# Interleaving the FFN weight tiles in pairs, so that TensorE loads its weights with a step of two elements

## The reference

```python
def swiglu(u, wg, wu, wd):
    return (jax.nn.silu(u @ wg) * (u @ wu)) @ wd      # u: 256 x 1024, wg, wu: 1024 x 2816, wd: 2816 x 1024
```

## Time and profile before

| what | value |
|---|---|
| median of three runs | 2071.14 us |
| the profiled execution, its own time | 2068.39 us |
| its span, first to last instruction | 2066.6 us |
| mean granted TensorE clock | 0.98 of full |
| TensorE matmuls / weight loads | 15720 / 15720 |
| VectorE busy | 1438.2 us (70%) |
| ScalarE busy | 1020.5 us (49%) |
| moved by DMA | 466.35 MB, mean 226 GB/s |

### The profile page before, as it was taken

One profiled execution on the slowest core, in us unless ns is written; L12 is line 12 of the kernel. 1 busy time (PEld: TensorE's weight loads), 2 busy tenths in 40 slices (PEclk: granted clock), 3 DMA queues, 4 the chain that ended last, 5 costly groups with the idle time before them and its releaser, 6 DMA issues.

```text
span 2066.6 us, 37422 instructions
## 1 busy us (share of the span) xinstructions
PE 1958.1 (95%) x15720; PEld 1905.4 (92%) x15720; DVE 1438.2 (70%) x2203; ACT 1020.5 (49%) x1568; POOL 116.3 (6%) x113
## 2 busy tenths in 40 slices
PE   3999899989999999999999979999999899999999
PEld 3999899989999999899899979998999898989998
DVE  5777687776676676968776757665677776756554
ACT  4454556454544444664545455453545454525553
POOL 0000002200000000022000010000000100000000
PEclk8999999999999999999999999999999999999999
DMA  8777565567776776755577746465578654554552
GB/s 348 271 270 281 196 237 197 185 215 255 255 285 211 251 274 224 260 188 215 185 284 268 282 171 217 158 219 209 202 265 284 231 205 164 206 192 176 200 190 99
DMA packets 83848, 466.35 MB, mean 226 GB/s; under 512 B 9440, under 2 KB 9568, under 8 KB 44512
## 3 DMA queue, kind: packets, MB, share of 16 engines
q1 hardware_dynamic: 46496, 326.00, 44.1%
q10 hardware_dynamic: 37184, 137.97, 18.6%
HBM read 462.88 MB, written 1.05 MB: 224 GB/s over the span
## 4 chain that ended last, share of the span: by engine, by line
PE 84%; DVE 8%; ACT 4%; DMA 2%; issue 1%; POOL 1%; ACTq 0%; DVEq 0%; SPq 0%
PE bank L646 83%; DVE low L1560 3%; DVE ada_ring L1542 1%; DMA region<-ada 1%; ACT high L1126 1%; DVE u_split L1603 1%; PE bank L915 1%; DVE tmp L1598 1%; DMA ring<-stream 0%; ACT u_split L1164 0%; POOL region L2046 0%; DVE region L1974 0%; DVE region L1929 0%; ACT rs L1147 0%; DVE region L1690 0%
## 5 line engine op out<-in xcount | busy, mean ns | idle before, releaser
L646 PE MATMUL bank<-u_split,high 128*128 128x256 f32 x6464 | 1147.9, 283 | 50.2 <-DVE u_split L1603 43.7
L646 PEld LDWEIGHTS bank<-u_split,high 128*128 128x128 f32 x6464 | 994.3, 190 | 61.1 <-DVE u_split L1603 36.6
L1560 DVE TENSOR_TENSOR low<-ring,high 128x1024 fp32r<-128x1024 f32 (+1 forms) x600 | 732.4, 1229 | 374.0 <-issue 224.0
L646 PE MATMUL bank<-u_split,low 128*128 128x256 f32 x3232 | 906.4, 280 | 0.0
L1126 ACT ACTIVATE high<-ring 128x1024 fp32r<-128x1024 f32 (+1 forms) x600 | 602.5, 1046 | 103.3 <-PE bank L646 87.7
L646 PEld LDWEIGHTS bank<-u_split,low 128*128 128x128 f32 x3232 | 615.3, 190 | 0.4
L646 PE MATMUL bank<-hid,high 128*128 128x256 f32 x2112 | 368.3, 279 | 0.0
L646 PEld LDWEIGHTS bank<-hid,high 128*128 128x128 f32 x2112 | 320.9, 188 | 0.0
L1542 DVE SCALAR_TENSOR_TENSOR ada_ring<-ada_ring,cond 128x1024 f32<-128x1024 f32 x242 | 298.1, 1233 | 0.0
L646 PE MATMUL bank<-hid,low 128*128 128x256 f32 x1056 | 295.0, 279 | 0.0
L646 PEld LDWEIGHTS bank<-hid,low 128*128 128x128 f32 x1056 | 200.4, 190 | 0.0
(11 more groups left out here) (186 smaller groups left out, 1642.3 us busy)
## 6 DMA issues: line engine op xcount, KB each, us to landing
ring<-stream SPq DMA_DIRECT2D x302, 1024.0 KB, 5.8
ada_ring<-ada ACTq DMA_DIRECT2D x242, 512.0 KB, 4.4
region<-ada ACTq DMA_DIRECT2D x7, 1024.0 KB, 22.3
ring<-stream SPq DMA_DIRECT2D x4, 640.0 KB, 4.2
region<-na_bias ACTq DMA_DIRECT2D x2, 1024.0 KB, 5.9
ring<-stream SPq DMA_DIRECT2D x4, 512.0 KB, 3.9
cst<-const ACTq DMA_DIRECT2D x1, 1600.0 KB, 21.1
cond<-cond SPq DMA_DIRECT2D x2, 512.0 KB, 7.5
```

The source lines that it names most:

```text
L646: return pe.e.matmul(out, lhs, rhs, start=start, stop=stop, skip_group_check=True)
L1560: dve.e.tensor_tensor(lo, src, hi.bitcast(F32), ALU.subtract).then_inc(*dve.done(("low", n)))
```

## The change

The two tiles 2j and 2j+1 of an FFN fill, which lay one behind the other, now lie woven: column 0 of the first, column 0 of the second, column 1 of the first, and so on. The host does this in `block`. The fills of FFN weights are marked `woven=True`; the fills of the mixers stay as they were. A tile is now read with the new view `Memory.woven(n, k)`: 128 elements at a step of two, starting at the pair's first or second element. The number, order, size and waits of all instructions on all engines and queues stay the same, and so do the sizes and the addresses of all transfers and buffers.

```diff
 class Fill:
-    def __init__(self, *parts):
-        self.parts = parts
+    def __init__(self, *parts, woven=False):
+        self.parts, self.woven = parts, woven
...
-        return np.concatenate(whole, axis=1).reshape(-1)
+        whole = np.concatenate(whole, axis=1)
+        if self.woven:
+            whole = whole.reshape(P, -1, 2, P).transpose(0, 1, 3, 2)
+        return whole.reshape(-1)
...
     def ffn(self, f, gate, up, down, layer, up_col):
         for n in range(FT):
-            both = self.fill_of((gate, layer, 0, KT, P * n, P), (up, layer, 0, KT, up_col + P * n, P))
+            both = self.fill_of((gate, layer, 0, KT, P * n, P), (up, layer, 0, KT, up_col + P * n, P), woven=True)
...
-            fill = self.fill_of(*tiles_[n:n + 2 * TILES])
+            fill = self.fill_of(*tiles_[n:n + 2 * TILES], woven=True)
...
+    def woven(self, n, k):
+
+        s = n % GRAINS * GRAIN + k // 2 * 2 * P
+        return [x[:, s:s + 2 * P].rearrange("p (n two) -> p two n", two=2)[:, k % 2, :] for x in (self.high, self.low)]
...
-                        t = mm3(b[:, i * T:(i + 1) * T], [x[:, k, :] for x in gs[i][1]], (m.uh[:, k, :], m.ul[:, k, :]),
+                        t = mm3(b[:, i * T:(i + 1) * T], m.woven(gs[i], k), (m.uh[:, k, :], m.ul[:, k, :]),
...
-                    t = mm3(b[:, i * T:(i + 1) * T], [x[:, k, :] for x in g], (m.uh[:, k, :], m.ul[:, k, :]),
+                    t = mm3(b[:, i * T:(i + 1) * T], m.woven(r, k), (m.uh[:, k, :], m.ul[:, k, :]),
...
-            t = mm3(b[:, 0:T], [x[:, at % TILES, :] for x in g], [x[:, k, :] for x in m.hid], k == 0, k == FT - 1)
+            t = mm3(b[:, 0:T], m.woven(r, at % TILES), [x[:, k, :] for x in m.hid], k == 0, k == FT - 1)
```

More of the change, by code:

```diff
@@ L126, in fill, with fill_of @@
         return self.fill_of(what)
-    def fill_of(self, *parts):
-        self.fills.append(Fill(*parts))
+    def fill_of(self, *parts, woven=False):
+        self.fills.append(Fill(*parts, woven=woven))
         return len(self.fills) - 1
@@ L741, in ffn @@
             if n == 0:
-                gs = [grain("gate", f, n), grain("up", f, n)]
+                gs = [grain("gate", f, n)[0], grain("up", f, n)[0]]
                 for k in range(KT):
@@ L745, in ffn @@
                     for i in range(2):
-                        t = mm3(b[:, i * T:(i + 1) * T], [x[:, k, :] for x in gs[i][1]], (m.uh[:, k, :], m.ul[:, k, :]),
+                        t = mm3(b[:, i * T:(i + 1) * T], m.woven(gs[i], k), (m.uh[:, k, :], m.ul[:, k, :]),
                                 k == 0 and i == 0, k == KT - 1)
-                t.then_inc(*pe.done(("read", gs[0][0]), ("read", gs[1][0]), ("full", "hid", f, n)))
+                t.then_inc(*pe.done(("read", gs[0]), ("read", gs[1]), ("full", "hid", f, n)))
                 continue
             for i, what in enumerate(("gate", "up")):
-                r, g = grain(what, f, n)
+                r, _ = grain(what, f, n)
                 for k in range(KT):
-                    t = mm3(b[:, i * T:(i + 1) * T], [x[:, k, :] for x in g], (m.uh[:, k, :], m.ul[:, k, :]),
+                    t = mm3(b[:, i * T:(i + 1) * T], m.woven(r, k), (m.uh[:, k, :], m.ul[:, k, :]),
                             k == 0, k == KT - 1)
@@ L758, in ffn @@
             if at % TILES == 0:
-                r, g = grain("down", f, at // TILES)
+                r, _ = grain("down", f, at // TILES)
             if k == 0:
```

## The result

The changed kernel takes 2112.52 us, the median of four runs (2111.83 to 2113.44 us). The kernel before took 2073.09 us in four runs beside it (2065.86 to 2075.61 us). The ratio is 1.0199, with a 95% interval from 1.0157 to 1.0241: slower by about 2%, clear of the noise. The time lies in the forecast range of 2050 to 2115 us, near its upper end, but that range was wide enough to take in a rival; the forecast itself, no change, was wrong.

The account below looks back on a forecast made before the run. The prediction took TensorE's pace in the six FFNs, load and matmul nearly balanced, as the bound. Four terms of 0 us left the profiled 2068.39 us, plus 2.75 us to the median: 2071 us, own range 2060 to 2082, with rivals 2050 to 2115.

Parts of the forecast that it names:

- parts (1) to (3): Host layout and transfers; the split on ScalarE and VectorE; queues, waits and matmuls: each forecast at 0 us.
- The two paces: FFN matmul pitches before the change: 5376 matmuls at the fast pace, 4128 at the slow one, 4.4 ns apart.
- The sum of 1093.6 us: Six unbroken TensorE runs in the chain, one per FFN, added up; more than half of the span.
- part (4): The 9504 FFN weight loads at a step of two: bounded from -18 to 1007 us, taken as 0.
- slack of 1 ns: In the FFNs at the fast pace, load alone 112.2 ns against matmul alone 113.3 ns per pitch.
- The second argument: FFN loads take elements at half the moving operand's rate, so a slower address step has room to hide.
- Rival A: FFN loads cost a few nanoseconds more and the slow pace holds everywhere: +24 us, 2095 us; chance 0.20.
- Rival B: FFN loads pay for skipped elements or no longer start beside the matmul before: +1007 us, about 3080 us; chance 0.10.
- Rival C: The FFNs' slow pace, if two reads meeting in memory, ends with another address order: -18 us, 2053 us; chance 0.24.

Follow-up runs that it names:

- down_woven: Changed kernel with only the down parts woven, gate and up dense as before: 2083.28 us, ratio 1.0087 to the kernel before.
- tiny_woven: Changed kernel with 24 extra matmuls of 32 columns ahead of each of two gate groups per FFN: 2166 us.
- some_woven: Changed kernel with the gate part of two hidden tiles per FFN split into matmuls of 128 columns: 2150 us.
- step3: Changed kernel with dense layout, each FFN load reading every third element, so products are of other weights: 2626 us.
- step4: Changed kernel with four tiles woven instead of two, so a load reads every fourth element: 3198 us.
- some_dense: Kernel before with the gate part of two hidden tiles per FFN split into matmuls of 128 columns: 2095 us.
- halves_dense: Kernel before with every FFN matmul of 256 columns split into two of 128, each with its own load: 5019 us.
- halves_woven: Changed kernel with every FFN matmul of 256 columns split into two of 128, each with its own woven load: 5022 us.

## Why the prediction was wrong

**What held.** TensorE's pace in the six FFNs is the whole matter. Layout, transfers, split, waits and queues cost nothing, as parts (1) to (3) had it: VectorE's busy time moved by 0.1 us, and in down_woven the dense parts kept their paces. Load and matmul run side by side and nearly at balance, 112 against 113.3 ns, so that "a nanosecond more per load costs up to 9504 x 0.001 = 9.5 us" was the right exchange rate. The two paces and their shares, 5376 and 4128, are those of the trace, and carried the account to 45.1 us of 45.0. The last 0.1 is partly luck, since the FFNs themselves grew by 44.3. The sum of 1093.6 us for the six FFNs misses the first 48 matmuls of two of them; it is 1107.7, and nothing in the forecast hangs on it.

**The step that failed** is part (4), "the value I take is 0, by the nearest row". The row was that the moving operand takes 1024 bytes in one pitch of 113.3 ns, and that a woven load spans the same. I named the load "another read path" and then gave it the moving operand's speed. The runs show the load's own: 64 pieces in 117.8 ns, in some stretches 120.0 (tiny_woven, some_woven), against 111.7 dense, and 1.8 to 1.9 ns for each further piece (step3, step4). The error is 4 to 7 ns above a pitch of 113, small as a rate and large against a slack of 1 ns (1.6 by the stretches of some_dense), which stood in the same paragraph. The second argument, that the load takes elements at 0.83 ns where the moving operand manages 0.44, counted elements, and what is paid for is pieces.

**Rival A** is what happened, and I had given it 0.20. Its place, the 0.11 us from a load's start to its matmul, was right. Its price of 24 us is what the woven load alone accounts for: its 117.8 ns happens to be the slow pace. The pitch went 2.2 ns beyond, to 120.0 in all of them, from a cause that stays open. By rival A's own rule that is 24 + 9504 x 0.0022 = 45 us. What should have raised its chance is that the range of unknown load costs, 0 to 107 ns, met a slack of 1 ns: only the lowest hundredth of it was free.

**Rival B**, half rate, did not happen at a step of two; a pitch near its 220 ns comes only at a step of four (235 ns). And its argument, that the load pays for what it skips, is half right at a step of two: the pieces are twice as many, but at 32 pieces they had cost less than the elements. **Rival C** had the sign wrong. The slow pace did go, but because a slower one took its place. Its support and rival A's, the reading of the earlier trace rows that the slow pace is a load that comes late, does not hold either: dense loads of 112 columns ran at 119 to 120 ns, slower than either pace, and one FFN of the dense 96-column run stayed near 117.7.

**A reading to mend.** I wrote that no wait stands between the fast and the slow pace in the earlier trace rows. No idle time is shown there, but the change falls on the 49th matmul of the down part, the first of a grain, where TensorE's program waits for the grain's low part (L655 of the kernel before) and, as for every tile, for a piece of `hid_low`. A wait that is already met shows no idle time. That the flips come from such waits is argued from their place alone; no run tests it.

**Lines and ports.** The note on 16-byte lines in the Trainium skill ("SBUF — State Buffer", Door 1: The DMA port swizzle) gives both halves that I set against each other. Full rate with two hits to a line, and a step of up to four fp32 elements as free, do not hold for this kernel's weight loads at the full clock: 118 to 120 ns at a step of two, 174 at three, 235 at four, against 111.7 dense. That each new line costs is what the runs show, and it can be seen as soon as the lines take longer than the elements. The statement of the Trainium skill ("TensorE: Matmul & The Clock Gate", Step-by-step: what each phase is for) that loads and moving operand have read ports of their own agrees with tiny_woven and some_woven in the main, 117.8 ns beside 32 columns and 117.8 or 120.0 beside 128. Beside 256 columns no run here shows whether the 2.2 ns are contention.

**What stays open.** What sets the last 2.2 ns of the woven pitch, nearly half of the loss. Why the dense kernel has two paces, and why shorter loads, woven or dense, have others between 113 and 120 ns. Several are steady over whole FFNs, so that they look like ways for two periodic streams to lock; no run here tests that. It also stays open whether the woven FFN would have gone back to 113.3 ns if its load alone had been under it.

## What to carry to other kernels

When a load of weights and a matmul of 256 columns are in balance, as here within 1 to 2 ns, the load's read pattern is part of the critical path. Keep weights dense, and price any step at the full clock by the 16-byte pieces it touches, about 1.8 ns each here, against 0.83 ns per element. Such a price is a floor: the pitch here went 2.2 ns beyond it. A rate borrowed from another port of the same engine may be off by a few per cent, which is all the slack that there is; when the cost is uncertain and the slack is nearly nothing, the likeliest outcome is not zero. And where a kernel has two paces, count how much of it runs in each before sizing an effect of a few nanoseconds, and time it in many runs: this one ranged from 2055.17 to 2083.46 us in thirteen.

## What the runs showed that I had not expected

**At the lower clock the step is free.** Matmuls near the start of the second FFN, in the kernel before and then in the changed one:

```profile
438.14 0.63 PE L646 MATMUL bank<-u_split,high 128*128 128x256 f32 x2
...
440.06 0.60 PE L646 MATMUL bank<-u_split,high 128*128 128x256 f32 x2
```

```profile
448.56 0.63 PE L655 MATMUL bank<-u_split,high 128*128 128x256 f32 x2
...
450.48 0.63 PE L655 MATMUL bank<-u_split,high 128*128 128x256 f32 x2
```

Nine matmuls take 1.92 us in both, 213 ns each, dense or woven. TensorE had idled for 2.7 us ahead of this FFN, and the granted clock in these rows is 0.50, the lower level (1.2 GHz). The better evidence is halves_dense and halves_woven at that level: their matmuls stream half as many columns, each load starts 0.11 us after the matmul before it, and the pitch is 213.3 ns in both.

**Splitting all FFN matmuls in two made the FFNs nearly four times as long.** In halves_dense there were twice as many, at a pitch of 213.3 ns instead of 113 to 118, with a mean granted clock of 0.587 where the kernel before had 0.98; the whole took 5019 us. In short stretches of the same form (some_dense), which came after full-length matmuls, the pitch was 112 ns and the clock stayed at 1.00.

**A shorter dense load can make a slower matmul.** 112 columns gave 119 to 120 ns, 96 columns 113 ns in five of six FFNs, 64 columns 119 ns in five of six, 8 columns 113 ns.
